# Two transformer blocks on one core: the feed-forward and the down projection multiply each high weight tile once, with the high and the low activations side by side as 512 moving columns

## The reference, cut to what matters

```python
def _swiglu(h, w_gate, w_up, w_down):
    return (jax.nn.silu(h @ w_gate) * (h @ w_up)) @ w_down
...
        h = _rms(x, ln2[l]) * (1 + sc2) + sh2
        x = x + g2 * _swiglu(h, w_gate[l], w_up[l], w_down[l])
```

## Time and profile before

| | us |
|---|---|
| median of three runs | 2565.42 |
| lowest, highest | 2555.59, 2568.86 |
| the profiled execution, its whole time | 2568.81 |
| its span from first to last instruction | 2567.0 |
| layer 0: hidden units, from the second on | 223.6 to 366.3 |
| layer 0: down units | 366.3 to about 430 |
| layer 1: hidden units, from the second on | 619.7 to 762.6 |
| layer 1: down units | 762.6 to about 826 |

### The profile page before, as it was taken

How to read it: one execution, slowest core, us unless ns; L and a number is a source line. 1 busy time by engine, 2 the same in 40 slices (tenths; PEclk the granted TensorE clock), 3 DMA queues, 4 the chain that set the end, 5 groups by cost and what they waited for, 6 DMA issues and landing times.

```text
span 2567.0 us, 43430 instructions
## 1 busy us (share of the span) xinstructions
PE 2372.8 (92%) x15400; PEld 2047.4 (80%) x15400; DVE 1220.7 (48%) x2236; ACT 1176.1 (46%) x2423; POOL 727.4 (28%) x563
## 2 busy tenths in 40 slices
PE   6989998989998899999987899999989999988998
PEld 3868898858898598878875578988769999857998
DVE  3663334664343624441158773154353642488353
ACT  3454454454454534442366652222343544567443
POOL 1403454413454121122222022212223223221433
PEclk8989999979999899999998999999999989999999
DMA  7755965755866121123211022212223334211544
GB/s 262 244 180 191 306 190 176 246 196 177 297 222 194 58 90 50 58 74 93 96 42 50 1 74 98 91 43 97 90 66 107 97 102 159 61 50 51 180 132 131
DMA packets 159782, 328.61 MB, mean 128 GB/s; under 512 B 17696, under 2 KB 21024, under 8 KB 159520
## 3 DMA queue, kind: packets, MB, share of 16 engines
q1 hardware_dynamic: 159504, 325.80, 39.4%
q0 software_dynamic: 144, 0.98, 0.1%
HBM read 325.67 MB, written 1.05 MB: 127 GB/s over the span
## 4 chain that ended last, share of the span: by engine, by line
PE 57%; issue 18%; DVE 11%; POOL 7%; ACT 3%; DMA 2%; POOLq 0%; SPq 0%; DVEq 0%; ACTq 0%
PE PS L1501 13%; PE PS L1502 13%; PE PS L1503 13%; POOL WL L1422 6%; PE PS L1525 3%; PE PS L1527 3%; PE PS L1526 3%; DVE BC L1247 2%; DMA RAW<-stream 1%; DVE WL L1996 1%; POOL AR L1442 1%; PE PS L486 1%; DVE WORK L1264 1%; PE PS L630 1%; ACT WH L1766 1%
## 5 line engine op out<-in xcount | busy, mean ns | idle before, releaser
L1422 POOL TENSOR_TENSOR WL<-RAW,WH 128x512 fp32r<-128x512 f32 x468 | 653.4, 1397 | 1657.6 <-ACT WH L1766 1657.2
L1501 PE MATMUL PS<-AR,WH 128*128 128x256 f32 (+1 forms) x2896 | 960.2, 332 | 56.5 <-DVE AR L2032 19.0
L1502 PE MATMUL PS<-AR,WH 128*128 128x256 f32 (+1 forms) x2896 | 939.6, 324 | 0.0
L1503 PE MATMUL PS<-AR,WL 128*128 128x256 f32 (+1 forms) x2896 | 938.2, 324 | 0.0
L1766 ACT ACTIVATE WH<-RAW 128x512 fp32r<-128x512 f32 x936 | 549.2, 625 | 420.8 <-PE PS L1503 230.8
L1996 DVE TENSOR_TENSOR WL<-RAW,WH 128x512 fp32r<-128x512 f32 x468 | 400.0, 856 | 623.0 <-ACT WH L1766 621.1
L1501 PEld LDWEIGHTS PS<-AR,WH 128*128 128x128 f32 x2896 | 562.7, 194 | 152.2 <-issue 79.4
L1502 PEld LDWEIGHTS PS<-AR,WH 128*128 128x128 f32 x2896 | 564.3, 195 | 41.4 <-issue 2.9
L1503 PEld LDWEIGHTS PS<-AR,WL 128*128 128x128 f32 x2896 | 563.1, 194 | 40.7
L1525 PE MATMUL PS<-WH,AR 128*128 128x256 f32 x768 | 226.1, 294 | 0.0
L1527 PE MATMUL PS<-WH,AR 128*128 128x256 f32 x768 | 219.1, 285 | 0.0
(11 more groups left out here) (253 smaller groups left out, 2776.4 us busy)
## 6 DMA issues: line engine op xcount, KB each, us to landing
RAW<-stream SPq DMA_DIRECT2D x936, 256.0 KB, 3.0
WORK<-mods SPq DMA_DIRECT2D x144, 512.0 KB, 6.1
C<-consts SPq DMA_DIRECT2D x1, 1088.0 KB, 8.6
XX<-xT SPq DMA_DIRECT2D x1, 1024.0 KB, 10.2
XX<-ctxT SPq DMA_DIRECT2D x1, 1024.0 KB, 5.9
outT<-XX SPq DMA_DIRECT2D x1, 1024.0 KB, 4.8
C<-consts POOLq DMA_DIRECT2D x1, 960.0 KB, 8.1
WORK<-lam SPq DMA_DIRECT2D x1, 256.0 KB, 3.6
```

The source lines that it names most:

```text
L1422: pool.tensor_tensor(WL[:, u % 4, cut, :], RAW[:, (2 * u + 1) % 4, :, :], WH[:, u % 4, cut, :].bitcast(f32), ALU.subtract).then_inc(lo_don ...
L1501: pe.matmul(out, WH[:, u % 4, k, :], moving[:, 0, k, :], start=(k == 0), stop=False)
L1502: pe.matmul(out, WH[:, u % 4, k, :], moving[:, 1, k, :], start=False, stop=False)
L1503: last = pe.matmul(out, WL[:, u % 4, k, :], moving[:, 0, k, :], start=False, stop=(k == KC - 1))
```

## The change

The two multiplies with the same high weight tile become one, whose moving operand is the high and the low activations of all tokens: 2 x 256 columns, written to the two halves of one bank. The low weight tile still multiplies the 256 high activations, into the first half. So the sum of a bank now lies in two halves, and whoever reads the bank adds them: in the hidden stage a DVE reduction (`tensor_reduce`, 512 in, 256 out) for each unit; in the down stage a second scaled addition to X. The sigmoid reads the sum that DVE has made (GATE 3) in place of PSUM.

```diff
+        def halves(bank):
+            return PS[:, bank, :].rearrange("p (s t) -> p s t", s=2)
+
+        def high_and_low(bank, u, k, moving, start, stop):
+            if start:
+                pe.matmul(halves(bank), WH[:, u % 4, k, :], moving, start=True, stop=False)
+            last = pe.matmul(PS[:, bank, 0:T], WL[:, u % 4, k, :], moving[:, 0, :], start=False, stop=False)
+            if not start:
+                last = pe.matmul(halves(bank), WH[:, u % 4, k, :], moving, start=False, stop=stop)
+            return last
...
                 pe.wait_ge(ff_done, l * FC + kk + 1 + BEGUN)
-                pe.matmul(PS[:, b, 0:T], WH[:, u % 4, k, :], HID[:, 0, kk, :], start=(kk == 0), stop=False)
-                pe.matmul(PS[:, b, 0:T], WH[:, u % 4, k, :], HID[:, 1, kk, :], start=False, stop=False)
-                last = pe.matmul(PS[:, b, 0:T], WL[:, u % 4, k, :], HID[:, 0, kk, :], start=False,
-                                 stop=(kk == FC - 1))
+                last = high_and_low(b, u, k, HID[:, :, kk, :], kk == 0, kk == FC - 1)
...
             def hidden(i, j):
-                done(b2, i, j)
                 if j % 2 == 0:
-                    act.activation(GATE[:, 0, :], PS[:, j, 0:T], ACT.Sigmoid).then_inc(ffsig, 1)
+                    act.wait_ge(bank_read[j], i + (earlier(b2 + j) + 1))
+                    act.activation(GATE[:, 0, :], GATE[:, 3, :], ACT.Sigmoid).then_inc(ffsig, 1)
                     next_high(b2, i, j)
...
             def hidden(b2, i, j):
+                done(b2, i, j)
+                x = (b2 - first) // 2 + j // 2
+                m = 2 * i + (l * FC + x + 1)
                 if j % 2 == 0:
+                    dve.wait_ge(ffu, m - 1 + BEGUN)
+                    dve.tensor_reduce(GATE[:, 3, :], both(j), AX.X, ALU.add).then_inc(bank_read[j], 1)
                     next_low(b2, i, j)
                 else:
-                    done(b2, i, j)
-                    x = (b2 - first) // 2 + j // 2
-                    m = 2 * i + (l * FC + x + 1)
                     dve.wait_ge(ff_done, m - 1 + BEGUN)
                     dve.wait_ge(ffsig, m)
-                    dve.tensor_tensor(GATE[:, 1, :], GATE[:, 0, :], PS[:, j - 1, 0:T], ALU.mult).then_inc(bank_read[j - 1], 1)
                     dve.wait_ge(bank_read[j - 1], i + (earlier(b2 + j - 1) + 1))
-                    dve.tensor_tensor(GATE[:, 2, :], GATE[:, 1, :], PS[:, j, 0:T], ALU.mult).then_inc(bank_read[j], 1)
+                    dve.tensor_tensor(GATE[:, 1, :], GATE[:, 0, :], GATE[:, 3, :], ALU.mult).then_inc(ffg, 1)
+                    dve.wait_ge(ffg, m)
+                    dve.tensor_reduce(GATE[:, 3, :], both(j), AX.X, ALU.add).then_inc(bank_read[j], 1)
+                    dve.wait_ge(bank_read[j], i + (earlier(b2 + j) + 1))
+                    dve.tensor_tensor(GATE[:, 2, :], GATE[:, 1, :], GATE[:, 3, :], ALU.mult).then_inc(ffu, 1)
                     next_low(b2, i, j)
...
-                    dve.scalar_tensor_tensor(X[:, bass.ds(k, 1), :], PS[:, bank:bank + 1, 0:T],
-                                             M1[:, l, bass.ds(40 + k, 1)], X[:, bass.ds(k, 1), :],
+                    x = X[:, bass.ds(k, 1), :]
+                    dve.scalar_tensor_tensor(x, PS[:, bank:bank + 1, 0:T], M1[:, l, bass.ds(40 + k, 1)], x,
+                                             ALU.mult, ALU.add).then_inc(ffd, 1)
+                    dve.wait_ge(ffd, 4 * i + (l * KC + j // 3 + 1))
+                    dve.scalar_tensor_tensor(x, PS[:, bank:bank + 1, T:2 * T], M1[:, l, bass.ds(40 + k, 1)], x,
                                              ALU.mult, ALU.add).then_inc(bank_read[bank], 1)
```

More of the change, by code:

```diff
@@ L267, in build @@
     sticks, wk_done = sem("sticks"), sem("wk_done")
-    ffg = sem("ffg")
+    ffg, ffu, ffd = sem("ffg"), sem("ffu"), sem("ffd")
     rot_done, cosd, rot_read = sem("rot_done"), sem("cosd"), sem("rot_read")
@@ L1504, in feature_unit, with hidden_unit @@
             last.then_inc(unit_done, 1)
+        def halves(bank):
[7 more added lines that the diff above has]
+            return last
+        def hidden_unit(base, i, j, ready):
+            u = unit_wait(base, i, j)
+            for k in range(KC):
+                pe.wait_ge(ready[0], ready[1] + k + 1)
+                last = high_and_low(u % 4, u, k, H1[:, :, k, :], k == 0, k == KC - 1)
+            last.then_inc(unit_done, 1)
         def token_pair(base, i, j, still, first, end, ready=None, only=None):
@@ L1739, in first_layer @@
             for j in range(2 * FF_STEPS):
-                feature_unit(b2, 0, j, H1, T, (norm_done, (2 * l + 1) * KC))
+                hidden_unit(b2, 0, j, (norm_done, (2 * l + 1) * KC))
                 if j % 2:
@@ L1744, in first_layer @@
             looped(pe, b4, FF_UNITS - 2 * FF_STEPS, 4,
-                   lambda i, j: feature_unit(b4, i, j, H1, T, (norm_done, (2 * l + 1) * KC)))
+                   lambda i, j: hidden_unit(b4, i, j, (norm_done, (2 * l + 1) * KC)))
             b3 = b2 + FF_UNITS
@@ L1965, in hidden @@
                     next_high(b2, i, j)
-                    act.wait_ge(bank_read[j], i + (earlier(b2 + j) + 1))
+                    act.wait_ge(ffu, 2 * i + (l * FC + j // 2 + 1 + BEGUN))
                     act.activation(HID[:, 0, bass.ds(2 * i + j // 2, 1), :], GATE[:, 2:3, :],
@@ L2319, in first_layer, with both @@
             b2 = first = b + WO_UNITS
+            def both(bank):
+                return PS[:, bank, :].rearrange("p (s t) -> p t s", s=2)
             def hidden(b2, i, j):
+                done(b2, i, j)
+                x = (b2 - first) // 2 + j // 2
+                m = 2 * i + (l * FC + x + 1)
                 if j % 2 == 0:
+                    dve.wait_ge(ffu, m - 1 + BEGUN)
+                    dve.tensor_reduce(GATE[:, 3, :], both(j), AX.X, ALU.add).then_inc(bank_read[j], 1)
                     next_low(b2, i, j)
                 else:
-                    done(b2, i, j)
-                    x = (b2 - first) // 2 + j // 2
-                    m = 2 * i + (l * FC + x + 1)
                     dve.wait_ge(ff_done, m - 1 + BEGUN)
                     dve.wait_ge(ffsig, m)
-                    dve.tensor_tensor(GATE[:, 1, :], GATE[:, 0, :], PS[:, j - 1, 0:T], ALU.mult).then_inc(bank_read[j - 1], 1)
                     dve.wait_ge(bank_read[j - 1], i + (earlier(b2 + j - 1) + 1))
-                    dve.tensor_tensor(GATE[:, 2, :], GATE[:, 1, :], PS[:, j, 0:T], ALU.mult).then_inc(bank_read[j], 1)
+                    dve.tensor_tensor(GATE[:, 1, :], GATE[:, 0, :], GATE[:, 3, :], ALU.mult).then_inc(ffg, 1)
[3 more added lines that the diff above has]
+                    dve.tensor_tensor(GATE[:, 2, :], GATE[:, 1, :], GATE[:, 3, :], ALU.mult).then_inc(ffu, 1)
                     next_low(b2, i, j)
@@ L2354, in first_layer @@
                 columns2()
-        for at, signal in enumerate((ff_done, gated, acc_done)):
+        for at, signal in enumerate((ff_done, gated, acc_done, ffu)):
             dve.memset(COL[:, 56 + at:57 + at], 0.0).then_inc(signal, BEGUN)
```

## The result

| | us |
|---|---|
| before, median (least to most) | 2559.27 (2553.47 to 2568.86) |
| after, median (least to most) | 2572.26 (2561.25 to 2580.22) |
| ratio, 95% interval | 1.0043 (1.0031 to 1.0055) |
| profiled execution after: span, whole | 2566.8, 2568.56 |

The change makes the kernel 0.43% slower, 11 us (the medians lie 13 us apart), where 9.6 us less was forecast. The two profiled executions don't show this in their spans (the one of before lies at the upper end of its own runs), so I compare stages, not spans. Windows over the same stages as in the earlier trace rows, after the change (columns as there): layer 0's hidden units with modulation, its last 12, its down units; then layer 1's hidden units with modulation and its last 12.

The account below looks back on a forecast made before the run. PE, busy throughout the hidden and down stages, was taken to bound the kernel. Savings of 5.2 us in layer 0 and 4.4 in layer 1 make 9.6, from a median of 2565.4 to 2556 us; range 2545 to 2567.

Parts of the forecast that it names:

- DVE, ACT, POOL ... So this costs nothing: Hidden and down units: added reductions, 1.4 us a pair, and second additions, 0.48 us a bank, stay covered and cost nothing.
- a lead of 5.65: Hidden units: low weights are ready 5.65 us before PE uses them; about 4.9 after the reduction, 2 us finally left.
- 31 us without cover: Hidden units: if the reductions were not covered, 0.7 us a pair would cost 31 us for 44 pairs.
- if PE waits on low parts of weights: Profile after: a sign, named in advance, that the forecast is wrong; no size given.
- The price of a chunk: Hidden and down matmuls: a chunk falls from 360 to 346 ns, saving 14, with bounds of 7 and 20.
- The middle way: Per chunk: 13 ns fixed per matmul, 120 ns for 256 columns and 227 for 512; one matmul fewer saves 13.
- layer 1's terms: Layer 1: 4.0 us from 14 hidden units and the down stage, plus 0.3 before; 4.3, or 4.4 with rounding.
- Layer 1's modulation weights hold 2.9 us: Layer 1's modulated hidden units: PE would be 3.2 us earlier, transfers leave 0.3, and PE waits the other 2.9.
- nothing is held back: Both layers: rival in which transfers start earlier and all 14.6 us come, or 20.8; 2551 to 2545 us, chance 0.18.
- Layer 0's down stage is paced by the ring: Weight slots for two units go round in 5.2 to 5.3 us against PE's 5.07, leaving 0.4 us saved there.
- The layers' ends hide the second addition: Ends of both layers: the extra 0.48 us a bank is hidden by later waits; uncovered it is 1.0 us.
- The slower rival: All chunks: uncovered weight loads when lengths alternate, starts 0.22 us apart, cost 89 us; 2655 us, chance 0.08.

Follow-up runs that it names:

- e1_pe_only: The changed kernel's matmuls, with sigmoid and products reading half a bank as before and no second addition in the down units; 2551.04 us, ratio 0.9968.
- e9_short_low: The changed kernel, with GpSimd making one chunk instead of four of each unit's low weights in the hidden units; 2550.03 us, ratio 0.9951.
- e12_one_addition: The changed kernel with one scaled addition a bank in the down units instead of two; 2569.04 us, ratio 1.0030.
- experiment 10: Two kernels: the change in the hidden units alone, 2563.81 us, ratio 1.0015; the change with one down-unit addition a bank, 2569.04 us, ratio 1.0030.
- (3): The changed kernel in full, with the two reductions writing their sums into free PSUM banks instead of SBUF; 2556.98 us, ratio 0.9974.

## Why the prediction was wrong

**The step that failed** is "DVE, ACT, POOL ... So this costs nothing". It cost the way from e1_pe_only's 0.9968 to the change's 1.0043, 19 us. Two things were wrong in it. First, the products were left out of the count: I priced what the diff adds, two reductions, which measured 682 and 692 ns as taken, and not what it moves. The change puts the products' second operand from PSUM to SBUF, and GpSimd then holds them up: 0.42 us became 1.04 and 0.86. None of these products had two SBUF operands before, but VectorE's low parts did, beside the same GpSimd, and in the trace of before they took up to 1.32 us in place of 0.69. The Trainium skill's page "SBUF — State Buffer", section "Who interferes with whom", has the rule. I had looked for the price of what was new only. Second, I let 0.7 us come off a lead of 5.65 once. The work comes again in every pair, and what matters is whether VectorE, ScalarE and the hand-overs between them get round in TensorE's time for a pair: 6.13 against 5.6. A lead covers a delay, not a rate. The bound that I gave for it, 31 us without cover, was of the right sign and never entered a rival. It also counted 0.7 us a pair where the text above it adds 1.4. The sign "if PE waits on low parts of weights" named the wrong value: what PE waited for was the low part of a hidden value, 2.1 and 1.8 us, and the modulation's weights.

**The price of a chunk.** Taken as 346 ns, measured 350 (0.23 + 0.12, and 351 from the down stage): inside the bounds of 340 and 353, 10 saved and not 14. On 1040 chunks that is 4 us less than forecast for the whole. (The middle way's own terms, 120 and 227, add up to 347, that is 13 saved; and layer 1's terms give 4.3 us, where the sum took 4.4.) The fixed 2.5 ns of the Trainium skill's page "TensorE: Matmul & The Clock Gate", Part 1, would give 2.6 us; e1_pe_only's 8 us and the table's 10 do not agree with it.

**Layer 1's modulation weights hold 2.9 us.** Wrong. PE waits for them in the changed kernel, 3.5 us, six times, which looks like a hit. In e1_pe_only and e9_short_low PE goes as fast or faster, the transfers take as long to land (6.6 us in the median in e1_pe_only and in the change), and the stage is 105.91 and 105.58 us, the full saving. The transfers are issued in SP's order behind weight transfers whose slots come free with the low parts. In layer 1 the first transfer of a step was issued 6.3 us on average (steps 3 to 16) behind PE's use of the step two before it, against 4.3 before the change and 4.5 in e1_pe_only. In the changed kernel VectorE's late low parts delay their issue; the earlier trace rows showed little room, not a limit of the transfers. The reading that "nothing is held back" was the right one for TensorE's part.

**Layer 0's down stage is paced by the ring.** Wrong. With hidden units as before, the stage is 61.90 us, and the landings are 2.9 us instead of the 3.2 of the earlier trace rows. Its 22 waits of before cost TensorE nothing, and they were no floor.

**The layers' ends hide the second addition.** Right as to its price (e12_one_addition: 1.0030 beside 1.0043, intervals that overlap). But the ends moved all the same, by 3.5 and 3.8 us, through the late weights (with one addition a bank by 1.5 and 3.4).

**The slower rival** named a gap of 0.22 us when lengths alternate. There is none. The kernel became slower by a mechanism to which I had given no chance.

**Range and sign.** The matmuls' part alone gave 8 us (e1_pe_only), near the 9.6 of the forecast, and that is luck: the chunk's price was 4 us too high, and 5 us were taken off for layer 0's ring and layer 1's transfers, neither of which held anything back there. So of the 20 us between the forecast change and the measured one, 19 are the failed step (with the second additions in it, whose share experiment 10 can't tell from nothing). The base of three runs, 2565.4, lay 6 us above the median of the 20 (2559.27), so the stated 2556 misses the measured time by 16 only. The profile leaves 4 of the measured 11 us unplaced.

The kernel with the sums in PSUM (3) beats both: 0.9974 of before, for the full computation.

## What to carry to other kernels

Price what a change moves as well as what it adds: an operand that goes from PSUM to SBUF makes another instruction of it if GpSimd works beside it, and how such an instruction fares may stand in the trace already, at another line. Where engines pass work round in a ring, compare the time of one round with the pace of the engine that must not wait; a lead is spent at the difference, each round. And when a transfer is late, look first at when it was issued.

## What the runs showed of the hardware that was not expected

- A VectorE product of 128x256 took 0.42 us with one operand in PSUM, whoever worked beside it (means of 414 to 422 ns in six kernels). With both in SBUF it took up to 1.54 us, and ended 0.28 us behind the GpSimd instruction inside which it began; where it began ahead of GpSimd's it took 0.42 as well. A low part of 128x512, both operands in SBUF, ended about 0.55 us behind where it was held up, in the kernel before too; with GpSimd's instruction cut from 1.35 to 0.51 us the two products took 0.44 and 0.53 on average.
- A reduction from PSUM into PSUM cost about as much as into SBUF: 696 and 699 ns against 682 and 692.
- 512 and 256 columns in alternation start 233 and 117 ns apart, 350 a pair, between the 340 and 353 that the passages in the earlier trace rows gave.
- Equal busy time of VectorE (28.1 us in the last 12 hidden units) went with ratios of 1.0009 and 1.0043: the busy time alone did not tell what VectorE's work cost the others.
